# A decoder-trunk kernel: a seventh slot for expert weights, one buffer of gathered rows, and overflow tables formed only inside the overflow branch

## What is computed

```
lg   = t @ w_rg + b_rg                    # 4 groups of experts; pick the best group
le   = (t @ w_re + b_re)[..., that group] # 8 experts in it; pick the best two
gate = softmax(top two) * softmax(lg)[that group]
a = einsum('td,edf->tef', t, w_gate)      # 32 experts, D_MODEL 1024, D_EXPERT 256
b = einsum('td,edf->tef', t, w_up)
y = einsum('tef,efd->td', silu(a) * b * comb, w_down);   x = x + y
```

## Time and profile before

| | |
|---|---|
| median of 3 runs | 1284.24 us (1281.35 to 1284.32) |
| the profiled execution: its own time | 1283.29 us |
| its span in the trace | 1281.5 us |
| TensorE busy | 1177.7 us, 92% of the span |
| VectorE busy | 695.8 us, 54% |
| ScalarE, POOL busy | 323.2 us, 146.8 us |
| DMA moved | 194.89 MB, of which 173.79 MB on SP's queue |

### The profile page before, as it was taken

One profiled execution on the slowest core, in us unless ns is written; L12 is line 12 of the kernel. 1 busy time (PEld: TensorE's weight loads), 2 busy tenths in 40 slices (PEclk: granted clock), 3 DMA queues, 4 the chain that ended last, 5 costly groups with the idle time before them and its releaser, 6 DMA issues.

```text
span 1281.5 us, 17642 instructions
## 1 busy us (share of the span) xinstructions
PE 1177.7 (92%) x6451; PEld 601.4 (47%) x6451; DVE 695.8 (54%) x2166; ACT 323.2 (25%) x934; POOL 146.8 (11%) x159
## 2 busy tenths in 40 slices
PE   6989879999999998998999999999768999999895
PEld 3435535545545555553555565555533334333231
DVE  1118689999999999631345454545553263222121
ACT  1133434344444448221111111111110010110000
POOL 0000000000000000300000000000001232333332
PEclk9997889999999999998999999999888999999998
DMA  8871000130001004267111011000658998999993
GB/s 316 307 246 40 1 1 25 44 121 34 20 15 34 12 14 171 99 222 282 34 50 47 3 50 50 34 1 34 268 220 347 393 340 311 331 379 381 391 354 65
DMA packets 48914, 194.89 MB, mean 152 GB/s; under 512 B 12240, under 2 KB 15094, under 8 KB 36515
## 3 DMA queue, kind: packets, MB, share of 16 engines
q1 hardware_dynamic: 37883, 173.79, 35.2%
q0 software_dynamic: 10368, 17.87, 5.9%
q10 hardware_dynamic: 576, 2.10, 0.4%
HBM read 172.60 MB, written 42.36 MB: 168 GB/s over the span
## 4 chain that ended last, share of the span: by engine, by line
PE 64%; DVE 22%; ACT 5%; issue 3%; DMA 3%; SPq 1%; POOL 0%; POOLq 0%; ACTq 0%; DVEq 0%
PE bank L835 15%; PE bank L1390 12%; DVE W L1891 11%; PE bank L1336 8%; PE bank L1397 7%; PE bank L1115 3%; PE bank L1314 3%; PE bank L1274 2%; PE bank L841 2%; PE bank L912 2%; PE bank L1377 2%; DMA W<-in_w_mv 1%; DVE G L1835 1%; DVE W L1941 1%; PE bank L896 1%
## 5 line engine op out<-in xcount | busy, mean ns | idle before, releaser
L835 PE MATMUL bank<-W,G 128*128 128x512 f32 (+1 forms) x768 | 314.6, 565 | 3.8 <-DVE G L1835 2.9
L1891 DVE SCALAR_TENSOR_TENSOR W<-W,dwT 128x128 f32<-128x128 f32 (+1 forms) x1048 | 271.7, 334 | 0.0
L835 PEld LDWEIGHTS bank<-W,G 128*128 128x128 f32 x768 | 145.4, 193 | 150.9 <-issue 147.5
L1390 PE MATMUL bank<-W 128*32 128x512 f32 x1344 | 171.7, 596 | 1.0 <-DVE W L2420 0.9
L1115 PE MATMUL bank<-W 128*128 128x512 f32 x256 | 113.3, 600 | 4.9 <-DVE W L2024 2.8
L1336 PE MATMUL bank<-W 128*128 128x512 f32 x256 | 115.2, 599 | 0.2 <-DVE W L2289 0.2
L708 POOL TENSOR_SCALAR st<-st 128x1 f32<-128x1 f32 (+3 forms) x40 | 13.8, 344 | 878.4 <-DVE st L1992 436.2
L2420 DVE TENSOR_TENSOR W<-bank,cvec 128x512 f32<-128x512 f32 x48 | 31.0, 686 | 132.4 <-PE bank L1377 132.4
L1390 PEld LDWEIGHTS bank<-W 128*32 128x32 f32 x1344 | 49.0, 111 | 106.1 <-issue 104.4
L1397 PE MATMUL bank<-W 128*32 128x512 f32 x672 | 87.3, 595 | 1.1 <-ACT W L1782 0.9
L1115 PEld LDWEIGHTS bank<-W 128*128 128x128 f32 x256 | 48.5, 192 | 63.5 <-issue 63.3
(11 more groups left out here) (358 smaller groups left out, 1512.7 us busy)
## 6 DMA issues: line engine op xcount, KB each, us to landing
W<-in_w_exp_gate SPq DMA_DIRECT2D x27, 1024.0 KB
W<-in_w_exp_up SPq DMA_DIRECT2D x27, 1024.0 KB
W<-in_w_exp_down SPq DMA_DIRECT2D x27, 1024.0 KB
W<-in_cache_mem_k SPq DMA_DIRECT2D x8, 1024.0 KB, 5.1
W<-in_cache_mem_v SPq DMA_DIRECT2D x8, 1024.0 KB, 7.5
W<-in_w_in SPq DMA_DIRECT2D x4, 1792.0 KB, 25.8
G<-in_w_exp_gate SPq DMA_DIRECT2D x5, 1024.0 KB
G<-in_w_exp_up SPq DMA_DIRECT2D x5, 1024.0 KB
```

The source lines that it names most:

```text
L835: mm = pe.matmul(bank[0:rows, at:at + hi - lo], HT[:, c, 0:rows], w[:, c, lo:hi], start=(c == 0), stop=(c == DC - 1))
L1390: mm = pe.matmul(B[2 + par][lo:hi, :], HG[par][:, c, lo:hi], WGU[u][:, :, c, :], start=(c == 0), stop=(c == DC - 1), skip_group_check=True)
L1891: dve.scalar_tensor_tensor(y, src, w, y, ALU.mult, ALU.add).then_inc(M["conv_tap"], 1)
```

## The change

The overflow tables and their matmuls move behind `If(total > 1)`; only the count is formed in every case. The room in G that the tables and the old `Z` and `HT` held, and that of `MKT` and `MV`, becomes slot 6 (gate/up in G 0 to 4095, down in G 10240 to 12287), and slot 5's down moves to G 8192 to 10239. The second row buffer becomes the third `YB`, and `ZG` is one buffer. SP loads slot 6 and slot 5's down once the last tile's probability-times-value matmuls are done. The gather of block n+1 is issued when block n's rows are turned.

```
-SLOTS, YBUFS = 6, 3
+SLOTS, YBUFS = 7, 3
-OVER_AT = 7
...
-        WGU.append(view(G, 4096, 2, DC, FE))
-        WD = [view(W, a, 2, D) for _, a in SLOT] + [view(W, 12288, 2, D), view(G, 2048, 2, D)]
-        ZG = [view(W, ROUT + 1024 * r, D) for r in range(2)]
+        WGU += [view(G, 4096, 2, DC, FE), view(G, 0, 2, DC, FE)]
+        WD = [view(W, a, 2, D) for _, a in SLOT] + [view(W, 12288, 2, D), view(G, 8192, 2, D), view(G, 10240, 2, D)]
+        ZG = view(W, ROUT, D)
...
-        YB = [view(W, ROUT + 4096 + 1024 * r, D) for r in range(2)] + [Z]
+        YB = [view(W, ROUT + 4096 + 1024 * r, D) for r in range(2)] + [view(W, ROUT + 1024, D)]
...
 # SP, cross-attention loop
+                if s2 == NT - 1:
+                    sp.wait_ge(M["pv2A_done"], AFTER["pv2A_done"] + NT - 1)
+                    sp.wait_ge(M["pv2D_done"], AFTER["pv2D_done"] + NT - 1)
+                    load_gate_up(sp, expert_id(NEED[6]), 6)
+                    load_down(sp, expert_id(NEED[6]), 6)
+                    load_down(sp, expert_id(NEED[5]), 5)
                 if 0 <= s2 < NT:
                     sp.wait_ge(M["x2_ready"], AFTER["x2_ready"] + 2 * s2 + 2)
...
-            for u in range(3, SLOTS):
-                if u == 5:
-                    for k in range(4):
-                        sp.wait_ge(x2_out[k], 16 * len(range(k, NT, 4)))
-                    sp.wait_ge(zg_in[0], 16)
-                    sp.wait_ge(zg_in[1], 16)
+            for u in range(3, 5):
                 load_gate_up(sp, expert_id(NEED[u]), u)
                 load_down(sp, expert_id(NEED[u]), u)
+            for k in range(4):
+                sp.wait_ge(x2_out[k], 16 * len(range(k, NT, 4)))
+            sp.wait_ge(zg_in, 16)
+            load_gate_up(sp, expert_id(NEED[5]), 5)
...
 # POOL
-            for n in range(2):
-                pool.wait_ge(M["route_ready"], n + 1)
-                gather(idx_i[:, BLOCKS[n]:BLOCKS[n] + 1], zg_in[n], ZG[n])
+            pool.wait_ge(M["route_ready"], 1)
+            gather(idx_i[:, BLOCKS[0]:BLOCKS[0] + 1], zg_in, ZG)
+            pool.wait_ge(M["route_ready"], 2)
             for n in range(NB + 3):
-                if n + 2 < NB:
+                if n + 1 < NB:
                     pool.wait_ge(M["zt4_done"], 2 * n + 2)
-                    at = BLOCKS[n + 2]
-                    gather(idx_i[:, at:at + 1], zg_in[n % 2], ZG[n % 2])
+                    at = BLOCKS[n + 1]
+                    gather(idx_i[:, at:at + 1], zg_in, ZG)
...
 # TensorE, expert_step(n)
-                    for mm in turn_rows(n, p, zg_in[p], (n // 2 + 2) * 16):
+                    for mm in turn_rows(n + 3):
...
-                if n == OVER_AT:
-
-                    pe.wait_ge(M["r_rows"], AFTER["r_rows"] + NT + 1)
-                    for k in range(2 * NT):
-                        mm = pe.matmul(B[5 - p][:, 256:256 + 2 * OVER], RRO[:, k, :], RQO[:, k, :, :], start=(k == 0), stop=(k == 2 * NT - 1))
-                    mm.then_inc(M["r_table"], 1)
...
+            pe.wait_ge(M["over_ready"], 1)
             total = pe.value_load(eid_i[0:1, OVER:OVER + 1], min_val=0, max_val=OVER + 1)
             with pe.If(total > 1):
+                pe.wait_ge(M["over_rows"], AFTER["over_rows"] + 1)
+                for k in range(2 * NT):
+                    mm = pe.matmul(B[5][:, 256:256 + 2 * OVER], RRO[:, k, :], RQO[:, k, :, :], start=(k == 0), stop=(k == 2 * NT - 1))
+                mm.then_inc(M["over_table"], 1)
...
 # VectorE: route_bases ends with the count, the rest moves to over_list()
+                dve.tensor_scalar(eid_i[:, OVER:OVER + 1], RBASE[:, 32:33], 1.0, 0.0, ALU.add, ALU.max).then_inc(M["over_ready"], 1)
...
-                route_rest(n)
+                if n == 0:
+                    route_counts()
+                if n == 2:
+                    route_bases()
...
             with dve.If(total > 1):
+                over_list()
```

More of the change, by code:

```diff
@@ L25 @@
 NB = NR
-EVEN = (NB + 1) // 2
 POS = 256
 SORT_TILE = 5
-SLOTS, YBUFS = 6, 3
+SLOTS, YBUFS = 7, 3
 PAD_TOK = 4096.0
-OVER_AT = 7
 DVE_TAPS = 23
@@ L281, in build @@
         RA = view(W, ROUT + 8136, NE)
-        _r = [0]
+        _r = [RMQ]
         def rt(*dims):
-            v = view(G, _r[0], *dims)
+            v = view(W, _r[0], *dims)
             _r[0] += int(np.prod(dims))
             return v
-        R_CNT, R_GT, ROV, RBASE = rt(1), rt(8), rt(128), rt(33)
-        R_ROOM = view(G, 9216 - 128, 128)
         R_RANK, R_EXP, R_BASE, R_FL, R_ROW, R_GATE = (rt(2 * NT) for _ in range(6))
         RE2, RG8, RE3, R_EID = rt(2 * NT, NE), rt(2 * NT, 8), rt(OVER, NE), rt(OVER)
-        R_TOK, R_FLAG, R_CAP = rt(OVER), rt(OVER), rt(NE)
+        R_TOK, R_FLAG = rt(OVER), rt(OVER)
         RE4 = RE3.rearrange("p k e -> p (k e)")[:, 0:2 * NT * NE].rearrange("p (t e) -> p t e", e=NE)
-        assert _r[0] <= 2048
-        RRO, RQO = view(G, 9216, 2 * NT, 128), view(G, 11520, 2 * NT, 2, OVER)
+        RRO, RQO = rt(2 * NT, 128), rt(2 * NT, 2, OVER)
+        assert _r[0] <= RMQ + 6144
+        ROV, R_ROOM = view(G, 12288, 128), view(G, 12416, 128)
+        R_CNT, R_GT, RBASE, R_CAP = view(G, 12708, 1), view(G, 12709, 8), view(G, 12717, 33), view(G, 12750, NE)
         LT, PAIR = view(G, 12544, 128), view(G, 12672, 36)
@@ L423, in build @@
             "r_taken": ("wout_in", 48),
+            "over_rows": ("uT_done", NT),
+            "over_table": ("uT_ready", NT),
+            "over_listed": ("u_ready", NT),
         }.items():
@@ L434, in build @@
         mk_in, mv_in = ring("mkb_in", 2), ring("mvb_in", 4)
-        wgu_in, zg_in, added = ring("wgu_in", SLOTS), ring("zg_in", 2), ring("added", YBUFS)
-        wdn_in = wmk_in + ring("wdn_in", SLOTS - 4)
-        WDN_AFTER = [16] * 4 + [0] * (SLOTS - 4)
+        wgu_in, zg_in, added = ring("wgu_in", 6) + [M["wmq_in"]], sem("zg_in"), ring("added", YBUFS)
+        wdn_in = wmk_in + ring("wdn_in", 2) + [M["wmo_in"]]
+        WGU_AFTER, WDN_AFTER = [0] * 6 + [64], [16] * 4 + [0] * 2 + [64]
         def adds_upto(n):
@@ L684, in _ @@
             with sp.If(total > 1):
+                sp.wait_ge(M["over_listed"], AFTER["over_listed"] + 1)
                 with sp.Fori(1, OVER + 1) as n:
@@ L787, in _ @@
                     add_block(n - 3)
-            pool.wait_ge(zg_in[0], 16 * EVEN)
+            pool.wait_ge(zg_in, 16 * NB)
             pool.wait_ge(M["zt4_done"], 2 * NB)
@@ L792, in _ @@
             with pool.If(total > 1):
+                pool.wait_ge(M["over_listed"], AFTER["over_listed"] + 1)
                 for n in range(NB - YBUFS, NB):
@@ L800, in _ @@
                     pool.sem_inc(M["gather_go"], 1)
-                    gather(idxs[:, 0:1], zg_in[0], ZG[0])
+                    gather(idxs[:, 0:1], zg_in, ZG)
                     pool.wait_ge(M["over_yA"], AFTER["over_yA"] + n)
@@ L1368, in _, with turn_rows @@
             place(B[6], 2 * NE)
-            def turn_rows(n, u, rows_in, count, banks=(0, 1)):
-                pe.wait_ge(rows_in, count)
+            def turn_rows(count):
+                pe.wait_ge(zg_in, 16 * count)
                 for half in range(2):
@@ L1376, in turn_rows @@
                         k = 4 * half + c
-                        mm = pe.transpose(B[half][:, c * 128:(c + 1) * 128], ZG[u][:, k * 128:(k + 1) * 128], ident)
+                        mm = pe.transpose(B[half][:, c * 128:(c + 1) * 128], ZG[:, k * 128:(k + 1) * 128], ident)
                     yield mm
@@ L1410, in expert_step @@
                     pe.wait_ge(M["hg_ready"], n * 2 + 4)
-                    weights_of(n + 1, wgu_in, 32, [0] * SLOTS)
+                    weights_of(n + 1, wgu_in, 32, WGU_AFTER)
                     if n:
@@ L1446, in _ @@
             pe.wait_ge(M["route_ready"], 2)
-            for mm in turn_rows(0, 0, zg_in[0], 16):
+            for mm in turn_rows(1):
                 mm.then_inc(M["zt4_done"], 1)
             pe.wait_ge(M["hg_ready"], 1)
-            weights_of(0, wgu_in, 32, [0] * SLOTS)
+            weights_of(0, wgu_in, 32, WGU_AFTER)
             gate_up(tiles_of(0), 0, 2).then_inc(M["gu_done"], 1)
-            for mm in turn_rows(1, 1, zg_in[1], 16):
+            for mm in turn_rows(2):
                 mm.then_inc(M["zt4_done"], 1)
@@ L1458, in _ @@
             pe.wait_ge(M["yb_readyD"], NB)
+            pe.wait_ge(M["over_ready"], 1)
             total = pe.value_load(eid_i[0:1, OVER:OVER + 1], min_val=0, max_val=OVER + 1)
             with pe.If(total > 1):
+                pe.wait_ge(M["over_rows"], AFTER["over_rows"] + 1)
+                for k in range(2 * NT):
+                    mm = pe.matmul(B[5][:, 256:256 + 2 * OVER], RRO[:, k, :], RQO[:, k, :, :], start=(k == 0), stop=(k == 2 * NT - 1))
+                mm.then_inc(M["over_table"], 1)
                 with pe.Fori(1, OVER + 1) as n:
-                    for mm in turn_rows(0, 0, zg_in[0], n * 16 + 16 * EVEN):
+                    for mm in turn_rows(n + NB):
                         mm.then_inc(M["over_t"], 1)
```

(14 more changed lines are left out.)

2 lines of the change are left out of this document (removed).

## The result

The median went from 1283.22 us (7 runs) to **1277.28 us** (7 runs, 1272.17 to 1279.20). The ratio is 0.9929, 95% interval 0.9904 to 0.9954; the two medians alone give 0.9954, the upper end of that interval. Two later sets with the same two kernels gave 0.9914 [0.9885, 0.9943] and 0.9913 [0.9884, 0.9941]. So the change is worth 0.5 to 0.9%. The forecast of 1273.5 us was 3.8 us low, inside its range.

The account below looks back on a forecast made before the run. TensorE's chain of 24 expert steps of 11.68 us was taken to bound the kernel, with DMAs also near full. Terms -3.96 - 1.38 - 6.90 + 0.3 + 1.2 + 0.6 = -10.1 us gave 1273.5 us, range 1269.5 to 1280.

Parts of the forecast that it names:

- (a): Overflow table matmuls on TensorE's chain in the expert stage: they go whole, since no row overflows, -3.96 us.
- (b): VectorE table work after steps 3 to 5, ahead of the next activation transposes: it goes, -1.38 us.
- (c): A long step from 1134.90 and the standstill at 1186.69 with its clock drop: waits for weights go, -6.90 us.
- The early loads: SP's loads at the last value matmuls: 4.2 MB fit the idle DMAs from 935 to 945, delaying writes without cost.
- The last gate_up: End of the expert stage: weights arrive 10.9 us earlier, 0.8 us late by the bound; no wait taken, upper end 4 us.
- A seventh slot can use a part: DMA share of 0.88 from 1040 to 1100: it leaves 7 us more, partly usable by a seventh slot.
- the weights bind again, later: Rival: DMAs idle 4 us more than counted, so the last gate_ups wait as long; 1277.5 us, chance 0.17.
- Turn 1: Transposes of block 1's gathered rows, behind the first gate_up: wait for the gather, 0.3 us taken, ends 0 to 3.5.
- Turn 2: Transposes of block 2's gathered rows near 989: wait for the gather's landing, 1.2 us, ends 0 and 3.0.
- Later turns: Row transposes in the steady steps: a gather may take 10.03 us, most cost nothing; 0.6 us in all, ends 0 and 12.
- The estimate by the Trainium skill: Gather time by a rule: 3.2 us for 0.52 MB, so no turn waits and the sum is -12.2 us; not followed.
- the rival by the Trainium skill: The single row buffer binds, gathers lengthen and turns wait: 1289.6 us, chance 0.05; a milder form 1279, chance 0.04.

Follow-up runs that it names:

- e3: The changed kernel with slot 6 and slot 5's down loaded last instead of at the value matmuls: 1282.65 us, ratio 0.9957 to the kernel before.
- e6: The kernel before with tables in the overflow branch, six slots, plus slot 5's down (1 MB) loaded at the value matmuls: 1279.37 us, ratio 0.9956.
- e2: The kernel before with the tables in the overflow branch and a single row buffer, still six slots: 1284.07 us, ratio 0.9972.
- e8: The changed kernel with one more semaphore that nothing uses: 1274.94 us, ratio 0.9917 to the kernel before.
- e1: The kernel before with only the tables moved into the overflow branch; six slots and two row buffers stay: 1280.59 us, ratio 0.9950.
- e4: The changed kernel with blocks 1 and 3 gathered into the third output buffer's room: 1278.40 us, ratio 0.9924 to the kernel before.
- e4_again: Repeat of e4, the changed kernel with blocks 1 and 3 gathered into the third output buffer's room: 1275.81 us, ratio 0.9925.
- e5: The changed kernel with two row buffers and two output buffers instead of one and three, seven slots: 1274.71 us, ratio 0.9924 to the kernel before.
- start-buffer form: The changed kernel with blocks 1 and 3 gathered into the third output buffer's room; e4, e4_again and one sharing an old semaphore: ratios 0.9924, 0.9925, 0.9921.
- e5_again: Repeat of e5, the changed kernel with two row buffers and two output buffers: 1277.35 us, ratio 0.9926 to the kernel before.
- a3: The changed kernel run again unaltered: 1275.49 us, ratio 0.9913 to the kernel before.

## Why the prediction was right or wrong

**(a), (b) right.** The matmuls gave -3.96, the VectorE work -1.44 for -1.38; from L1428 to L1428 it is 11.68 us in each of steps 3 to 7.

**(c) right in size, half right in cause.** All 6.90 us went. But I let the early transfer of 4.2 MB pay for it ("if the weights come early enough"). e3 shows that the seventh slot alone removes the standstill, e6 that 1 MB of head start without it does nothing for the stage. A larger head start with six slots was not tried.

**The early loads, right.** They went out at 932.10, the DMAs carried 406 GB/s between 935 and 945, and the y and z writes behind them (948.96, 952.39) cost nothing that can be seen in the stage; the first gather left at 968.43.

**The last gate_up: the step that failed.** "I take no wait, with 4 us as the upper end": it was 1.22 us, 1.43 with the slower start of the step, and 1.05 to 1.55 in every kernel with seven slots, an early load and three output buffers. The working moved the weights' arrival by the whole 10.9 us of the head start. Of this, 3.3 us went into the stop at 1064, and 3.9 us into another, behind the first seven slots' loads at 981.4 (SP next issues at 984.35). e3, which has neither stop, started its last gate_up only 2.6 us later than the changed kernel: that is what a head start of 10.9 us was worth there. The two stops leave 3.7 us, so about 1 us stays unexplained. "A seventh slot can use a part" of the spare share was the sentence to work out: the share of 1040 to 1100 rose only from 0.88 to 0.91. The rival "the weights bind again, later" (0.17) had the mechanism, loads that stand idle longer than counted; its price was 4 us and the measured one 1.4. That its 1277.5 lies closer to the measured median than the forecast is chance: by the stage, -8.0 lies midway between the forecast's -10.1 and this rival's -6.1.

**Turn 1.** 0.3 taken, 0 measured in the changed kernel, but 1.18 in e2 and 1.66 in e3, inside the ends of 0 to 3.5. That gather took 6.3 us in the changed kernel, by the semaphore's updates, and 8.3 and 9.1 in e2 and e3. e3 differs from the changed kernel only in the order of the loads, so the wait was saved because the loads beside that gather had gone out early. The prediction had not counted this.

**Turn 2, right.** 1.2 us predicted, 1.01 of wait and 1.23 in the step found here (waits of 0.77 and 0.85 in the repeats, 1.03 in e8), released by the gather's DMA, at 993.99: 989.16 plus the 3.7 us of scatter plus the wait.

**Later turns.** 0.6 us taken, 1.8 measured: 1.3 at turn 4, whose gather took 11.09 us, longer than any landing before, and 0.5 in three more steps. The prediction's "All 24" was read too widely: the trace times 12 of the 24 landings in that row. The repeats waited 0.62 and 0 us at turn 4, and their steps sum to 1.4 and 0.2 us for this term, so its size is in part the chance of one execution. The median gather took 9.0 us by the semaphore's updates, near the 8.8 of before as I had argued, and the row buffer did not bind in the steady steps. "The queue states stay as they were" was too strong for the gathers of the first steps. The estimate by the Trainium skill, "DMA: Bandwidth & Descriptors", section "Anatomy of one DMA", by which the sum would have been -12.2, was not borne out: the shortest gather after took 4.5 us against its 3.2.

**The sum.** Predicted -10.1, found -8.0 in the stage: +1.4 for the last gate_up, +1.2 for later turns, -0.3 for turn 1, the rest in tenths. Against the rival by the Trainium skill, "Trainium Kernel Development and Optimization", section "Best Practices": double-buffering the rows is worth 2.8 us with six slots (e1, e2); with seven it gave 2.5 to 2.9 us on TensorE in e4 and e4_again, and 0.4 and 1.0 us at the end of the span, less than the intervals can tell. Paid for with the third output buffer (e5) it gave nothing.

## What to carry to other kernels

Where compute and transfers both run near full, follow the transfers as a chain of their own: find the last moment at which the loading queue stands for want of a free buffer, and count from there. A head start ahead of that moment is lost as far as the queue then stands still; more buffer depth, or reaching that moment earlier, is not. Price each part of such a trade by a kernel of its own, as the sum (-3.9, +2.8, -6.9) hides that one part is a loss, and price it again beside the other parts: with seven slots it was 2.5 to 2.9 us on TensorE, of which at most 1.0 us showed at the end of the span.

## What the runs showed of the hardware that I had not expected

GpSimd's closing drain is part of the measured time and differs between programs that do the same work: 3.42 us in the changed kernel, its repeats, e2, e3 and e8, 3.62 in the kernel before, e1, e5 and e6, 5.79 in all three runs of the start-buffer form, each time to the hundredth. What sets it stays open. The granted clock fell to its lower level (1.2 GHz) after TensorE had stood for 4.74 (before), 4.65 (e1), 3.29 (e5_again), 3.22 (e2), 2.96 (e5) and 2.79 us (e3), after 2.21 us in e6 but not after 2.10 us in the same run, and in e3 after 1.66 us with 0.94 us soon behind it but not after 1.89 us in e1. In a3 it fell near the end after 1.45 and 0.47 us, where TensorE stands as long in every run and the last down is slowed in no other. In the records it stayed down for 3.4 us each time. A gate_up behind it took 8.77 us instead of 6.87 or 7.07, a down 5.3 instead of 3.6.
